# Streaming matmul columns in interleaved pieces of 16, with the split weights moved by 128 bytes

## The reference

```python
for l in range(DEPTH):                       # first block, 2 layers
    h = rmsnorm(x, norm_mix_pre[l]);  proj = h @ w_in[l]        # 1024 x 7168
    ...                                      # retention, two causal convolutions, gates
    x = x + rmsnorm(merged @ w_o[l], norm_mix_post[l])
    h = rmsnorm(x, norm_ffn_pre[l]);  up = causal_dwconv(h @ w_up[l], ffn_conv_w[l])
    gate, val = jnp.split(up, 2, axis=-1)
    x = x + rmsnorm((jax.nn.silu(gate) * val) @ w_down[l], norm_ffn_post[l])
for l in range(DEPTH):                       # second block, 2 layers
    proj = rmsnorm_2(x, pre_norm_g[l]) @ w_in[l]                # 1024 x 10432
    ...                                      # spatial gating, latent attention, RG-LRU
    x = x + rmsnorm_2(merged @ w_out[l], post_norm_g[l])
```

## Time and profile before

| | |
|---|---|
| median of 3 runs | 3190.64 us (3190.47 to 3191.49) |
| the profiled execution | 3190.44 us, of which the span from the first to the last instruction is 3189.1 us |
| TensorE matmul | 3169.5 us busy, 99%, 14964 matmuls |
| LDWEIGHTS | 2654.6 us busy, 83%, 14964 |
| VectorE | 1835.7 us busy, 58% |
| ScalarE | 1243.9 us busy, 39% |
| GpSimd | 396.0 us busy, 12% |
| DMA | 107 GB/s on average |

### The profile page before, as it was taken

How to read it: one execution, slowest core, us unless ns; L and a number is a source line. 1 busy time by engine, 2 the same in 40 slices (tenths; PEclk the granted TensorE clock), 3 DMA queues, 4 the chain that set the end, 5 groups by cost and what they waited for, 6 DMA issues and landing times.

```text
span 3189.1 us, 37007 instructions
## 1 busy us (share of the span) xinstructions
PE 3169.5 (99%) x14964; PEld 2654.6 (83%) x14964; DVE 1835.7 (58%) x2469; ACT 1243.9 (39%) x1866; POOL 396.0 (12%) x293
## 2 busy tenths in 40 slices
PE   8999999999999999999999999999999999999999
PEld 7888888888888888888888888888888888888887
DVE  6875456665687545656557543447545754345744
ACT  3332334344333233434445422236534442224642
POOL 0201212210020121211011000110012000011001
PEclk9999999999999999999999999999999999999999
DMA  4322223235442222323532222222232132222222
GB/s 167 116 99 93 99 93 112 94 132 188 139 125 93 99 93 100 106 97 119 194 125 78 97 99 87 97 86 98 97 122 87 67 104 94 86 99 95 92 94 101
DMA packets 100232, 339.71 MB, mean 107 GB/s; under 512 B 12288, under 2 KB 12544, under 8 KB 99296
## 3 DMA queue, kind: packets, MB, share of 16 engines
q1 hardware_dynamic: 96736, 322.76, 29.8%
q0 software_dynamic: 3184, 14.06, 1.3%
q10 hardware_dynamic: 144, 0.52, 0.1%
HBM read 326.29 MB, written 2.10 MB: 103 GB/s over the span
## 4 chain that ended last, share of the span: by engine, by line
PE 97%; DVE 1%; issue 1%; ACT 0%; DMA 0%; POOL 0%; POOLq 0%
PE ps L500 96%; PE ps L605 1%; PE ps L844 0%; DVE r L1427 0%; DVE wl L1417 0%; DMA X<-x_in 0%; POOL sm L2020 0%; ACT f L1265 0%; DVE h L1560 0%; DVE sm L1853 0%; PE ps L555 0%; DVE f L1553 0%; DVE f L1803 0%; DVE f L1863 0%; DVE r L1835 0%
## 5 line engine op out<-in xcount | busy, mean ns | idle before, releaser
L500 PE MATMUL ps<-h,wh 128*128 128x512 f32 (+1 forms) x5824 | 1702.5, 376 | 2.2 <-DVE h L1560 1.8
L500 PEld LDWEIGHTS ps<-h,wh 128*128 128x128 f32 x5824 | 1066.8, 189 | 199.3 <-issue 4.6
L500 PE MATMUL ps<-h,wl 128*128 128x512 f32 (+1 forms) x2912 | 1093.2, 375 | 0.0
L1417 DVE TENSOR_TENSOR wl<-raw,wh 128x1024 fp32r<-128x1024 f32 (+3 forms) x596 | 751.8, 1272 | 319.6 <-ACT wh L957 318.7
L957 ACT CAST wh<-raw 128x1024 fp32r<-128x1024 f32 (+3 forms) x596 | 595.9, 1008 | 720.1 <-PE ps L500 718.3
L500 PEld LDWEIGHTS ps<-h,wl 128*128 128x128 f32 x2912 | 548.7, 188 | 98.8
L500 PE MATMUL ps<-r,wh 128*128 128x512 f32 x1632 | 503.8, 390 | 0.0
L500 PEld LDWEIGHTS ps<-r,wh 128*128 128x128 f32 x1632 | 305.2, 188 | 62.7
L500 PE MATMUL ps<-r,wl 128*128 128x512 f32 x816 | 317.5, 389 | 0.0
L1032 ACT CAST r<-f 128x512 fp32r<-128x512 f32 x186 | 114.6, 620 | 511.9 <-DVE f L1756 148.5
L500 PE MATMUL ps<-wh,r 128*128 128x512 f32 x960 | 302.6, 390 | 0.3
(11 more groups left out here) (152 smaller groups left out, 2085.9 us busy)
## 6 DMA issues: line engine op xcount, KB each, us to landing
raw<-wst SPq DMA_DIRECT2D x544, 512.0 KB, 3.3
raw<-wst SPq DMA_DIRECT2D x48, 320.0 KB, 2.8
f<-gains POOLq DMA_DIRECT2D x6, 1024.0 KB, 5.2
raw<-wst SPq DMA_DIRECT2D x16, 384.0 KB, 3.0
f<-f SPq DMA_DIRECT2D x72, 64.0 KB, 2.0
f<-tab POOLq DMA_DIRECT2D x16, 256.0 KB, 5.0
r<-r SPq DMA_DIRECT2D x32, 128.0 KB, 2.3
X<-x_in SPq DMA_DIRECT2D x4, 512.0 KB, 8.4
```

The lines of the kernel that those rows point to most:

```text
L500: return e.matmul(o, a, b, start=start, stop=stop, skip_group_check=True)
L1417: e.tensor_tensor(l[:, 0:WIDTH[c]], raw[:, c % NRAW, 0:WIDTH[c]], h[:, 0:WIDTH[c]].bitcast(F32), ALU.subtract).then_inc(*lo_cut.up(("lo", c)))
```

## The change

Matmuls of `three` that use ring weights take their moving operand and their PSUM tile in another order of columns: 16 columns (64 bytes) of the first half of the tile, the same 16 of the second half, then the next 16 of the first, and so on. All operands of the three matmuls are reordered alike, so the same numbers land at the same places. `KEPT` chunks and the attention scores keep the plain order. Matmuls that don't go through `three` (the retention, values, transposes and small ones) are as before. `WAY` goes from 48 to 80, which puts `wh` and `wl` at 128 modulo 256 (64 + 320 = 384).

```diff
-WAY = 48
+WAY = 80
...
+def paced(a):
+
+    return a.rearrange("p (u c e) -> p c u e", u=2, e=16)
...
-            def three(o, ah, al, bh, bl, start, stop):
+            def three(o, ah, al, bh, bl, start, stop, order=paced):
+                o, bh, bl = order(o), order(bh), order(bl)
                 mm(o, ah, bh, start, False)
                 mm(o, ah, bl, False, False)
                 return mm(o, al, bh, False, stop)
+
+            def plain(a):
+                return a
...
-            def rows_by(B, t, n, ks, xs, h, l, cols, last_k, closes=None):
+            def rows_by(B, t, n, ks, xs, h, l, cols, last_k, closes=None, order=paced):
...
-                                 k == 0, k == last_k)
+                                 k == 0, k == last_k, order)
...
-                    rows_by(B, t, n, (2 * c, 2 * c + 1), xs, h, l, (0, S), 7, name if t == 3 else None)
+                    rows_by(B, t, n, (2 * c, 2 * c + 1), xs, h, l, (0, S), 7, name if t == 3 else None,
+                            plain if NAME[name] in KEPT else paced)
...
-                        three(o[:, 0:n], R(55)[:, b], R(56)[:, b], R(57)[:, 0:n], R(58)[:, 0:n], True, False)
+                        three(o[:, 0:n], R(55)[:, b], R(56)[:, b], R(57)[:, 0:n], R(58)[:, 0:n], True, False, plain)
```

## The result

The changed kernel takes 3347.93 us (median of 4 runs, 3347.46 to 3349.19) against 3190.57 for the kernel before: a ratio of 1.0493, interval 1.0475 to 1.0511. It is slower by 157.4 us. I had forecast 3050 us.

What follows compares the result with a forecast made beforehand. TensorE's matmul pace was taken as the bound: 134.9 us less at 512 columns and 9.2 at 256, sum 144, less 4 given back, makes 140 off 3190.4, so 3050 us; range 3020 to 3225.

Steps and rivals of the forecast that it cites:

- What bounds the kernel: TensorE busy 3169.5 of 3189.1 us, so the kernel gets shorter only if matmuls follow each other faster.
- the 13.4 ns: Time each 512-column matmul takes over its columns, 226.7 against 213.3 ns; put down to the weight load running beside it.
- the gain of 11.2 ns a matmul: 512-column ring matmuls going from 226.7 to 215.5 ns, 12,048 of them, 134.9 us less.
- two streams meeting in the same part of memory: Hypothesis: at full rate the moving operand's SBUF stream repeatedly overtakes the weight load's, modulo 256, causing the loss.
- The half-rate rows: Matmuls at 1.2 GHz or with plain float32 lose next to nothing beside a load; taken as support for meeting streams.
- The row against it: At 2217.17 a matmul with no load beside it still took 0.39 us, as long as its neighbours.
- the case that rests on it: Rival: the loss comes from elsewhere than the load and nothing changes, 3190 +- 6 us; chance 10%.
- the give-back: 4 us added for splits or PSUM releases coming a little late at layer boundaries.
- the stretch from 43 to 163 us: VectorE's densest stretch, 101.8 of 120 us busy; it would bound only if more than 18% were saved, against 5%.
- The jumps cost: Rival: one cycle for each of 31 jumps between pieces, 163 us more, 3353 us; large loss 16%, small 10%.
- 16 columns are long runs: The argument given against the rival that jumps between pieces cost time.
- The address: Moving the ring by 128 bytes (`WAY`): cost put at nothing, covered by VectorE's 58% and ScalarE's 39%.

Runs made afterwards that it cites:

- moving_only: The changed kernel with only the moving operand read in pieces and the PSUM tile written in plain order; 3347.77 us.
- pieces_load_one: The changed kernel with `WAY` 48 and each three's stationary operand its first column 128 times, so loads read one address; 3347.66 us.
- way48_paced: The changed kernel with the ring back at its old place (`WAY` 48), columns still in pieces; 3347.53 us, ratio 1.0490.
- moving_one: The kernel before with every moving operand of a three replaced by its first column repeated, so the stream reads one address; 3051.42 us.
- load64: The kernel before with 64 instead of 128 stationary columns in the second and third matmul of each three; 3217.73 us.
- load_one: The kernel before with each three's stationary operand its first column 128 times, so every load reads one address; 3231.65 us.
- way80_plain: The kernel before with only the ring's new place (`WAY` 80), all columns in plain order; 3258.39 us, ratio 1.0211.
- psum_only: The changed kernel with only the PSUM tile taken in pieces and the moving operand read in plain order; 3256.99 us.

## Why the prediction was wrong

**What bounds the kernel** was right: TensorE's pace alone, with 12,048 and 1,152 matmuls. 12,048 x 13.3 ns closes the sum of what was lost to 2%.

**The step that failed is what the 13.4 ns are, and with it the gain of 11.2 ns a matmul that the order was to bring.** I read from equal losses at 512 and 256 columns, and from none at half rate, that "two streams meeting in the same part of memory" make them, and that a stream whose place modulo 256 advances at half rate would meet the load no more: 215.5 ns. The runs show 240.2 ns, and that the load has no part in the slowdown: the moving operand's order alone makes the whole slowdown (`moving_only`), and with that order the load's walk and its place are indifferent (`pieces_load_one`, `way48_paced`). What I took for pacing is what makes the stream dear. In plain order, too, what lowers the distance of 512-column matmuls is one address instead of a walk of the stream, 215.9 ns with the load unchanged (`moving_one`); half a load and a load that stands still bring nothing (`load64`, `load_one`).

At 256 columns in plain order the load does count: standing still it takes the distance from 120 to 113.3 ns, of the 111.7 that `moving_one` reaches there (24 matmuls in 34.15 - 31.47 = 2.68 us). So the 13.3 ns of both widths, which I took for one cost, answer to different things. The half-rate rows fit both readings, since at half rate a stream has twice the time for each read; they couldn't tell them apart, and I used them as if they could.

**The row against it was the right one for 512 columns.** The matmul with no load beside it that took 0.39 us I called the strongest row against my reading, and then gave the case that rests on it 10%, since durations vary from 388 to 398 ns. The variation is real, but says nothing of a load. The case itself, that nothing changes, didn't come true either.

**The size of the gain, had there been one,** was well judged in its pace: `moving_one` has 215.9 ns where I took 215.5, and 111.7 with 256 columns where I took 112. That it ends at 3051.4 us against my 3050 is in part luck: it also speeds up the `r,r` matmuls, which the change leaves alone (382 against 391 ns, 576 of them, 5 us), and of the give-back, 4 us, its page shows more: 3050.1 less 3022.7 us busy are 27.4 us idle, 8 more than before. One reading in the sum's surroundings was off: in the stretch from 43 to 163 us VectorE leaves 18.2 of 120 us free, which is 15% and not 18%; with 5% to be saved it changes nothing.

```profile
PE 3022.7 (99%) x14964; PEld 2660.0 (87%) x14964; DVE 1833.0 (60%) x2469; ACT 1240.4 (41%) x1866; POOL 393.8 (13%) x293
```

**The rival that came true in its time, not in its reason.** "The jumps cost", at a cycle each, gave 3353 us; measured 3348. But its own rule fails at 256 columns (15 jumps at no cost on average), at 7 jumps (no cost) and at 63 (17 ns for 26), and PSUM's jumps cost nothing. I left it out of the range with 16%, and that was the mistake in the range: with a reading that one row contradicts, the unpriced cost of an order of reads never seen in the trace should have had more weight than "16 columns are long runs".

**The address** I costed at nothing on its own, and named no case for it. It costs 67 us in plain order (`way80_plain`) and nothing more with the changed order.

**Ports and patterns.** The Trainium skill says that a load takes no bandwidth from the running matmul ("TensorE: Matmul & The Clock Gate", "Step-by-step: what each phase is for"). The runs with the changed order agree (`pieces_load_one` and `way48_paced`, 3347.7 and 3347.5 us). In plain order the traces differ: the ring's place alone costs 5.7 ns a matmul, and at 256 columns a load that stands still saves 6.7. The Trainium skill also says that any non-contiguous pattern in PSUM slows matmuls significantly ("Advanced Engine Details and Errata", "PSUM Cachelines"). That doesn't show for runs of 64 bytes: `psum_only` takes 3257.0 us and the plain order at the same place 3258.4.

**What stays open.** Why a plain walk costs 13 ns a matmul; why 256 columns lose as much as 512, yet a load that stands still brings half of it back there and nothing at 512; why four pieces 512 bytes apart are cheaper than two 1024 apart; and how the load's place enters in plain order. That the read order makes the slowdown is shown; by which addresses it does so is not, and I have no rule that gives all the distances.

## What to carry to other kernels

When the bound is TensorE's pace, the order in which float32r columns are read from SBUF is worth per cents in both directions: measure it, with the moving operand pinned to one address as the run that shows how much there is to win at all. A loss that vanishes at half rate doesn't say which of two readers makes it; runs that hold one reader still at a time do, and only for the width and the order in which they were made. And when a row contradicts the mechanism that a forecast rests on, the forecast's chance has to go down with it, and the costs of what the trace has never shown have to stay in the range.

## What the runs showed of the hardware

- A float32r matmul of 512 columns follows the last after 215.9 ns when its moving operand stays within 16 bytes, 226.7 in plain order, 240.2 in pieces of 64 bytes from two halves, and 242.0 when it goes round in 64 bytes.
- In plain order a load that reads one address takes 256-column matmuls from 120 to 113.3 ns and 512-column ones from 227 to 231.4; with the changed order it moves neither.
- PSUM written in pieces of 64 bytes from two halves in turn costs nothing beside the plain order.
- The place of the split weights against the activations, 0, 128 or 64 modulo 256, makes 3190, 3258 and 3261 us in plain order, at equal work.
- With 16-byte pieces 64 bytes apart single matmuls come down to the length of one that reads one address, others in the same sequence don't; the mean is 0.6% better over the kernel.
